# Choosing the first gather unit of a PEER layer in stages: best expert alone, then eight, then the rest

## The chip, the cores and the metric

The kernel runs on one core of one Trainium2 chip. The metric is the device time of one execution in microseconds (us); the median of three executions stands for the kernel. One execution was taken by the hardware profiler; its trace gives every number below. The engines are TensorE (PE in the profile), VectorE (DVE), ScalarE (ACT), GpSimd (POOL) and the queue engine SyncE (SP), and 16 DMA engines move data.

## The reference

The program computes two layers of a transformer trunk on 256 tokens of width 1024. Layer 0 mixes the tokens with a 2-D neighbourhood attention, layer 1 with a latent attention. After each mixer stand a layer norm and a product-key expert layer (PEER), then another layer norm. The expert layer is what matters here. For each token and each of 8 heads:

```
q = x @ w_q                       # two halves of 128
s = q . sub_keys                  # 2 x 128 scores
sv, si = top_k(s, 16)             # 16 best keys of each half
cand_s = sv[0][:, None] + sv[1][None, :]          # 16 x 16 sums
cand_i = si[0][:, None] * 128 + si[1][None, :]
best_s, pos = top_k(cand_s, 16)
e_idx = cand_i[pos]               # 16 experts of 16384
gate = softmax(best_s)
hid = gelu(x . u[e_idx])
y += sum(gate * hid * v[e_idx])
```

So each token of each layer reads 8 x 16 = 128 rows u and 128 rows v of a large table.

## The kernel before

The 256 tokens are two tiles of 128, one token to a partition. A group g is one head of one tile: 16 groups in a layer, 16 rows k in each, so 512 gathers in all (`row_no` numbers them). One gather (L1073, GpSimd, an indirect DMA) fetches for each of 128 tokens one expert's u and v, 8 KB a partition, 1.05 MB in all, into one of `RING` = 8 slots of the tile `uv`.

For every row VectorE computes the dot product with the token (`dot`, L1621, it reads `px` in PSUM), ScalarE applies Gelu to the results of two rows (`weigh`), VectorE multiplies by the gate (`weights`, L1627), ScalarE builds a diagonal matrix (L1228), and TensorE adds diagonal times v to the sums (`add`, L638). Three rows of group 0 (k = 5, 9, 13), and some of later groups, are added by VectorE instead (`add_on_vector`). A gather into a slot waits until the row eight before it has been added (`s_acc`, or `s_vrow`). In layer 0 the slots hold attention weights first, so the gathers n < 5 also wait for the projection "rest" n of TensorE (`rest_of_keys`, L362, and `rest_of_queries`, L370), and gather 7 waits for `rest_of_keys(6)` (`s_k6`).

There is no planner. Each engine has its own program, and within an engine the order is the order of the text. Pieces of side work (`side`) are tied to row numbers. VectorE chooses the experts of group g + 1 between the dots of group g: `key_top16` at one row, `pair_top16` two rows later, `expert_numbers` two after that, `gates` two after that. Group 0 of a layer has no rows to hide behind. `first_tile` does it in one piece: layer norm, `key_top16` (it waits for ScalarE's copy of the scores, `store_key_scores`, L1185), `pair_top16` (with the numbers of the first eight experts inside it), `expert_numbers` of the other eight, `gates`, and in layer 1 the rotation of the queries (`rope_q`, L1596).

The choice works so. MAX8 finds the eight largest of a row, FIND_INDEX8 their places, MATCH_REPLACE8 puts -1e30 over them, and a second MAX8 finds the next eight. The place `pos` of a pair in the 16 x 16 square is split into its two coordinates; each is compared with 0..15 (`hit`), the hits are multiplied by the key numbers and summed (`pick`), and first times 128 plus second plus the layer's offset is the expert's number.

GpSimd waits on `s_top8` before the gathers k = 0..7 of group 0 and on `s_top` before k = 8. In `first_tile(0)` TensorE's order is: rest 0, transposes of the norm, rest of keys 1, queries of group 0 (L536), half a seed (L348), key scores of group 0 into PSUM bank 7 (L548), rest of queries 1, rest 2 to 4, seed, `load_px` (L523), queries and key scores of group 1 (bank 7 again), rest of keys 6; then the rows. In layer 1 it is: queries 0, half a seed, key scores 0, two rotated-query products, seed, queries and scores of groups 1 and 2, `load_px`.

## Time and profile before

| | us |
|---|---|
| median of 3 executions | 1594.32 |
| lowest, highest | 1591.54, 1594.63 |
| profiled execution, its own time | 1593.75 |
| its span in the trace | 1591.9 |
| busy: PE, DVE, ACT, POOL | 1351.2, 1064.4, 488.0, 494.5 |
| first gather of layer 0, last of layer 0 | 125.63, 814.85 |
| first gather of layer 1, last of layer 1 | 904.56, 1568.51 |

The span counts from the first to the last instruction of the trace; the time of the execution is 1.85 us more. All times inside the program are from the span's start. "DMA share" is the mean busy share of the 16 DMA engines, "PEclk" the granted clock of TensorE as a part of 2.4 GHz.

### The profile page before, as it was taken

How to read it: one execution, taken by the hardware profiler on the slowest of the kernel's cores; microseconds unless marked ns; L12 is line 12 of the kernel's file. 1: busy time of each engine (PE TensorE's matmuls, PEld its weight loads, DVE VectorE, ACT ScalarE, POOL GpSimd, SP SyncE). 2: the span in 40 equal slices, each digit the busy share in tenths (PEclk: the TensorE clock that was granted, in tenths of full speed). 3: DMA queues.
4: the chain of work that ended last, by engine and by line, in shares of the span. 5: the costliest groups of instructions: out<-in, count | busy, mean ns of one | idle time of the engine just before them, and what ended most of it. 6: DMA issues, size and time to landing. Idle time of an engine off the chain costs nothing.

```text
span 1591.9 us, 16214 instructions
## 1 busy us (share of the span) xinstructions
PE 1351.2 (85%) x5046; PEld 733.5 (46%) x5046; DVE 1064.4 (67%) x2835; ACT 488.0 (31%) x1274; POOL 494.5 (31%) x524
## 2 busy tenths in 40 slices
PE   7999888888887888789889879988778988887877
PEld 7888534433354454444446634444334443333322
DVE  1127876778867877676653587777875876776765
ACT  1122342334323332223334233343332322222222
POOL 0003333334333333333320133343333333333331
PEclk9999998989998999999999989999999999999999
DMA  9528999999999999999993499999999999999996
GB/s 353 188 102 322 399 408 421 409 414 411 409 410 403 422 417 422 418 421 385 406 388 106 171 416 420 408 411 419 407 390 420 414 402 421 420 421 422 421 421 268
DMA packets 92821, 601.20 MB, mean 378 GB/s; under 512 B 10432, under 2 KB 12864, under 8 KB 26560
## 3 DMA queue, kind: packets, MB, share of 16 engines
q0 software_dynamic: 73728, 536.90, 82.2%
q1 hardware_dynamic: 19008, 63.28, 10.5%
q8 instruction: 40, 0.66, 0.2%
q14 instruction: 45, 0.37, 0.1%
HBM read 599.09 MB, written 1.05 MB: 377 GB/s over the span
## 4 chain that ended last, share of the span: by engine, by line
PE 37%; DMA 33%; DVE 22%; issue 3%; ACT 3%; DVEq 2%; POOL 0%; SPq 0%; POOLq 0%
DMA uv<-in_peer_uv_dram,expert 32%; PE y L638 19%; DVE uv L1621 11%; PE spare L536 3%; PE y L500 3%; PE px L353 2%; PE y L378 2%; ACT diag L1228 1%; DVE key_idx L1511 1%; DVE key_left L1503 1%; DVE key_idx L1505 1%; PE spare L395 1%; DVE wts L1627 1%; DVE key_top L1500 1%; DVE pos L1528 1%
## 5 line engine op out<-in xcount | busy, mean ns | idle before, releaser
L638 PE MATMUL y<-uv,diag 128*128 128x512 f32 x1888 | 912.9, 623 | 167.7 <-ACT diag L1228 166.9
L1621 DVE CUSTOM_DVE_ANT_0 uv<-px,uv 128x1024 f32<-128x1024 f32 x512 | 617.5, 1220 | 305.8 <-DMA uv<-in_peer_uv_dram,expert 299.6
L1073 POOL DMA_INDIRECT uv<-in_peer_uv_dram,expert x512 | 491.0, 959 | 1064.0 <-PE y L638 838.4
L638 PEld LDWEIGHTS y<-uv,diag 128*128 128x128 f32 x1888 | 349.5, 197 | 610.1 <-issue 341.6
L1228 ACT ACTIVATE diag<-ident,wts 128x128 f32<-128x128 f32 x472 | 166.3, 394 | 440.1 <-DVE wts L1627 430.9
L1220 ACT ACTIVATE act_hid<-hid 128x2 f32<-128x2 f32 x260 | 52.9, 203 | 482.4 <-DVE hid L1621 482.0
L1220 ACT ACT_TABLE_LOAD x54 | 69.3, 1283 | 1.0
L477 PE MATMUL spare<-ident,probs 128*128 128x128 f32 x96 | 16.9, 302 | 39.2 <-DVE probs L1448 35.8
L1640 DVE SCALAR_TENSOR_TENSOR vsum<-uv,wts,vsum 128x1024 f32<-128x1024 f32 x37 | 47.5, 1284 | 3.8 <-issue 0.5
L1627 DVE TENSOR_TENSOR wts<-act_hid,gate 128x2 f32<-128x2 f32 x260 | 40.6, 156 | 12.5 <-ACT act_hid L1220 12.4
L1621 DVE DVE_READ_ACCUMULATOR2_ANT hid<- 128x1 f32 x512 | 42.3, 83 | 0.0
L1190 ACT ACT_TABLE_LOAD x30 | 38.5, 1283 | 0.5
L1392 DVE TENSOR_TENSOR probs<-spare,bias 128x320 f32<-128x320 f32 x16 | 7.6, 473 | 45.4 <-PE spare L395 45.4
L477 PEld LDWEIGHTS spare<-ident,probs 128*128 128x128 f32 x96 | 11.4, 150 | 53.1 <-DVE probs L1448 52.5
L536 PEld LDWEIGHTS spare<-hT,wb_rows 128*128 128x128 f32 x256 | 30.6, 192 | 6.1 <-issue 6.1
L536 PE MATMUL spare<-hT,wb_rows 128*128 128x128 f32 x256 | 31.8, 277 | 0.0
L353 PE MATMUL px<-hT,uv 128*128 128x160 f32 (+1 forms) x176 | 24.6, 300 | 8.0 <-DMA uv<-in_na_w_dram 8.0
L500 PE MATMUL y<-wb_rows,oT 128*128 128x512 f32 x64 | 30.1, 592 | 0.0
L353 PEld LDWEIGHTS px<-hT,uv 128*128 128x128 f32 x176 | 24.1, 201 | 9.6 <-issue 9.6
L548 PEld LDWEIGHTS spare<-keysT,qT 128*128 128x128 f32 x128 | 18.7, 191 | 13.5 <-issue 11.5
L1540 DVE TENSOR_TENSOR hit<-pos_abf,iota 128x512 f32<-128x512 f32 (+1 forms) x34 | 22.5, 661 | 2.9 <-issue 0.4
L1543 DVE TENSOR_TENSOR hit<-hit,key_idxf 128x512 f32<-128x512 f32 (+1 forms) x34 | 22.5, 661 | 2.5
(268 smaller groups left out, 1272.6 us busy)
## 6 DMA issues: line engine op xcount, KB each, us to landing
uv<-in_peer_uv_dram,expert POOLq DMA_INDIRECT x512, 10.8
wb_rows<-in_peer_w_q_dram SPq DMA_DIRECT2D x16, 512.0 KB, 8.7
uv<-in_na_w_dram SPq DMA_DIRECT2D x11, 512.0 KB, 9.9
wb_rows<-in_na_w_out_dram SPq DMA_DIRECT2D x8, 512.0 KB, 9.0
uv<-in_mla_w_out_dram SPq DMA_DIRECT2D x8, 512.0 KB, 10.7
wb_rows<-in_mla_w_out_dram SPq DMA_DIRECT2D x8, 512.0 KB, 7.8
bias<-in_na_bias_dram SPq DMA_DIRECT2D x16, 160.0 KB, 7.5
w_vu<-in_na_w_dram SPq DMA_DIRECT2D x4, 512.0 KB, 8.6
```

Of the source, the lines that this page charges most:

```text
L353: last = T.matmul(B[b][:, 0:width], w[:, k, :], hT[:, k, 0:width], start=(k == 0), stop=(k == DK - 1))
L378: last = T.matmul(B[3][:, t * P:(t + 1) * P], hT[:, k, t * P:(t + 1) * P], w[:, k, :], start=(k == 0), stop=(k == DK - 1))
L500: last = T.matmul(Y[t][:, c, :], oT[n % 2][:, :], w[:, c * 512:(c + 1) * 512], start=False, stop=(j == PAIRS - 1))
L536: last = T.matmul(B[b][:, c * DKEY:(c + 1) * DKEY], w[:, k, :], hT[:, k, t * P:(t + 1) * P], start=(k == 0), stop=(k == DK - 1))
L638: last = T.matmul(Y[t][:, c, :], diag[:, n % RING, :], uv[:, n % RING, 1, c * 512:(c + 1) * 512], start=False, stop=(k == TOPK - 1 and g % ...
L1073: pool.indirect_dma_start(uv[:, n % RING, :, :].rearrange("p h d -> p (h d)"), None, uv_table, bass.IndirectOffsetOnAxis(ap=expert[:, g, k ...
L1190: A.activation(best_e[:, :], best_d[:, :], ACT.Exp).then_inc(s_be, 1)
L1220: A.activation(act_hid[:, first:end], hid[:, first:end], ACT.Gelu).then_inc(s_gelu, 1)
L1228: A.activation(diag[:, n % RING, :], ident[:, :], ACT.Copy, scale=wts[:, k:k + 1]).then_inc(s_diag, 1)
L1621: V_.tensor_tensor_reduce(out=rows, in0=px[:, :, :], in1=rows, scale=1.0, scalar=0.0, op0=ALU.mult, op1=ALU.add, accum_out=hid[:, k:k + 1] ...
L1627: V_.tensor_tensor(wts[:, first:end], act_hid[:, first:end], gate[:, g, first:end], ALU.mult).then_inc(s_wts, 1)
L1640: V_.scalar_tensor_tensor(out=vsum[:, :], in0=rows, scalar=wts[:, k:k + 1], in1=vsum[:, :], op0=ALU.mult, op1=ALU.add).then_inc(s_vrow, 1)
```

## The change

Group 0 of each layer is chosen by a new function, `first_choice`, that reads the key scores straight from PSUM bank 7. It is in stages. The eight best keys of each half are found, and with them the best pair, which is always the best key of one half with the best of the other: its number is stored and `s_best` raised, on which gather k = 0 now waits. Then the best eight pairs are sought in the 8 x 8 square of these keys, their numbers decoded with comparisons 8 wide, and `s_top8` raised for k = 1..7. After that bank 7 is given back, the second eight keys are found, the 16 x 16 square is made with the taken pairs covered, and the other eight pairs chosen. ScalarE's copy of group 0's scores is gone. For all groups the decoding is shorter: the multiplication by 128 and the offset are applied to the key numbers at once (`key_numbers`), the coordinates are compared as integers with no cast in between, and one sum over both halves gives the expert's number.

```diff
@@ -47,6 +47,7 @@
 START = 4
 QUADS = HEADS // 4
 FIRST = 204
+TOP = 8
 THROUGH = 6
 KEPT = 6
 SPAN = 160
@@ -158,9 +159,8 @@
         best = sb("best", [P, TOPK])
         pos = sb("pos", [P, TOPK], u32)
         pos_ab = sb("pos_ab", [P, 2, TOPK], u32)
-        pos_abf = sb("pos_abf", [P, 2, TOPK])
-        hit = sb("hit", [P, 2, TOPK, TOPK])
-        pick = sb("pick", [P, 2, TOPK])
+        hit = sb("hit", [P, TOPK * 2 * TOPK])
+        pick = sb("pick", [P, TOPK])
         best_d = sb("best_d", [P, TOPK])
         best_e = sb("best_e", [P, TOPK])
         ahead = sb("ahead", [P, 16])
@@ -203,7 +203,7 @@
         s_first_half = sem("first_half_of_sums_done"); s_var = sem("ln_var_ready"); s_std = sem("ln_std_ready"); s_xhat = sem("ln_xhat_ready")
         s_css = sem("latent_squares"); s_cstd = sem("latent_std"); s_cn = sem("latents_normed")
         s_q0 = sem("first_half_of_queries_done"); s_px = sem("px_ready")
-        s_bd = sem("best_minus_max"); s_be = sem("best_exp"); s_top = sem("experts_chosen"); s_top8 = sem("first_experts_chosen")
+        s_bd = sem("best_minus_max"); s_be = sem("best_exp"); s_top = sem("experts_chosen"); s_top8 = sem("first_experts_chosen"); s_best = sem("top_expert_chosen")
         s_uv = [sem(f"expert_rows_landed{i}") for i in range(RING)]
         s_dot = sem("dot_done"); s_gelu = sem("gelu_done"); s_wts = sem("weights_ready")
         s_vrow = sem("v_row_added_by_vector")
@@ -1057,10 +1057,12 @@
                     if g:
                         pool.wait_ge(s_top, layer * GROUPS + g + 1)
                     else:
-                        pool.wait_ge(s_top8, layer + 1)
+                        pool.wait_ge(s_best, layer + 1)
                     for k in range(TOPK):
                         n = row_no(layer, g, k)
-                        if g == 0 and k == 8:
+                        if g == 0 and k == 1:
+                            pool.wait_ge(s_top8, layer + 1)
+                        if g == 0 and k == TOP:
                             pool.wait_ge(s_top, layer * GROUPS + 1)
                         if n >= RING and row_on_vector(n - RING):
                             pool.wait_ge(s_vrow, vrow_no(n - RING + 1))
@@ -1313,7 +1315,6 @@
                     store_rest(0)
                 fetch_table(ACT.Exp)
                 store_queries(layer, 0, 6)
-                store_key_scores(layer, 0, 7)
                 if layer == 0:
                     store_rest(1)
                     store_rest(2)
@@ -1510,17 +1511,22 @@
                 for c in range(2):
                     V_.max_index(key_idx[:, c, 8:16], key_top[:, c, 8:16], key_left[:, c, :])
 
-            def pair_top16(layer=None):
-                V_.tensor_tensor(cand[:, :, :], key_top[:, 0, :].unsqueeze(2).broadcast_to([P, TOPK, TOPK]),
-                                 key_top[:, 1, :].unsqueeze(1).broadcast_to([P, TOPK, TOPK]), ALU.add)
-                V_.tensor_copy(key_idxf[:, :, :], key_idx[:, :, :])
+            def key_numbers(layer, some):
+                V_.tensor_scalar(key_idxf[:, 0, some], key_idx[:, 0, some], float(KEYS), float(layer * EXPERTS), ALU.mult, ALU.add)
+                V_.tensor_copy(key_idxf[:, 1, some], key_idx[:, 1, some])
+
+            def pair_sums(out, n):
+                V_.tensor_tensor(out, key_top[:, 0, 0:n].unsqueeze(2).broadcast_to([P, n, n]),
+                                 key_top[:, 1, 0:n].unsqueeze(1).broadcast_to([P, n, n]), ALU.add)
+
+            def pair_top16(layer):
+                pair_sums(cand[:, :, :], TOPK)
+                key_numbers(layer, slice(0, TOPK))
                 flat = cand[:, :, :].rearrange("p a b -> p (a b)")
                 dve.drain()
                 V_.max(best[:, 0:8], flat)
                 dve.drain()
                 V_.max_index(pos[:, 0:8], best[:, 0:8], flat)
-                if layer is not None:
-                    expert_numbers(layer, 0, slice(0, 8), s_top8)
                 V_.match_replace(cand_left[:, :], best[:, 0:8], flat, NEG)
                 dve.drain()
                 V_.max(best[:, 8:16], cand_left[:, :])
@@ -1529,25 +1535,62 @@
                 V_.tensor_tensor(best_d[:, :], best[:, :], best[:, 0:1].broadcast_to([P, TOPK]), ALU.subtract)\
                   .then_inc(s_bd, 1)
 
-            def expert_numbers(layer, g, some=slice(0, TOPK), done=s_top):
+            def expert_numbers(g, some, width, skip, done):
                 n = some.stop - some.start
-                dve.drain()
-                V_.tensor_scalar(pos_ab[:, 0, some], pos[:, some], 4, None, ALU.logical_shift_right)
-                V_.tensor_scalar(pos_ab[:, 1, some], pos[:, some], TOPK - 1, None, ALU.bitwise_and)
-                dve.drain()
-                V_.tensor_copy(pos_abf[:, :, some], pos_ab[:, :, some])
-                dve.drain()
-                V_.tensor_tensor(hit[:, :, some, :], pos_abf[:, :, some].unsqueeze(3).broadcast_to([P, 2, n, TOPK]),
-                                 iota16[:, :].unsqueeze(1).unsqueeze(1).broadcast_to([P, 2, n, TOPK]), ALU.is_equal)
-                dve.drain()
-                V_.tensor_tensor(hit[:, :, some, :], hit[:, :, some, :],
-                                 key_idxf[:, :, :].unsqueeze(2).broadcast_to([P, 2, n, TOPK]), ALU.mult)
-                dve.drain()
-                V_.tensor_reduce(pick[:, :, some], hit[:, :, some, :], X, ALU.add)
-                dve.drain()
-                V_.tensor_scalar(pick[:, 0, some], pick[:, 0, some], float(KEYS), float(layer * EXPERTS), ALU.mult, ALU.add)
-                dve.drain()
-                V_.tensor_tensor(expert[:, g, some], pick[:, 0, some], pick[:, 1, some], ALU.add).then_inc(done, 1)
+                hits = hit[:, 0:n * 2 * width].rearrange("p (n c a) -> p n c a", n=n, c=2)
+                dve.drain()
+                V_.tensor_scalar(pos_ab[:, 0, some], pos[:, some], 4 if width == TOPK else 3, None, ALU.logical_shift_right)
+                V_.tensor_scalar(pos_ab[:, 1, some], pos[:, some], width - 1, None, ALU.bitwise_and)
+                dve.drain()
+                V_.tensor_tensor(hits, pos_ab[:, :, some].rearrange("p c n -> p n c").unsqueeze(3).broadcast_to([P, n, 2, width]),
+                                 iota16[:, 0:width].unsqueeze(1).unsqueeze(1).broadcast_to([P, n, 2, width]), ALU.is_equal)
+                dve.drain()
+                V_.tensor_tensor(hits, hits, key_idxf[:, :, 0:width].unsqueeze(1).broadcast_to([P, n, 2, width]), ALU.mult)
+                dve.drain()
+                V_.tensor_reduce(pick[:, some], hits.rearrange("p n c a -> p n (c a)"), X, ALU.add)
+                dve.drain()
+                chosen = slice(some.start + skip, some.stop)
+                V_.tensor_copy(expert[:, g, chosen], pick[:, chosen]).then_inc(done, 1)
+
+            def first_choice(layer):
+                scores = [B[7][:, c * KEYS:(c + 1) * KEYS] for c in range(2)]
+                block, rest = vsum[:, 0:TOP * TOP], vsum[:, TOP * TOP:2 * TOP * TOP]
+                dve.wait_ge(s_full[7], job["ks", layer, 0])
+                for c in range(2):
+                    V_.max(key_top[:, c, 0:8], scores[c])
+                dve.drain()
+                for c in range(2):
+                    V_.max_index(key_idx[:, c, 0:8], key_top[:, c, 0:8], scores[c])
+                pair_sums(block.rearrange("p (a b) -> p a b", a=TOP), TOP)
+                dve.drain()
+                key_numbers(layer, slice(0, TOP))
+                V_.max(best[:, 0:8], block)
+                dve.drain()
+                V_.tensor_tensor(expert[:, 0, 0:1], key_idxf[:, 0, 0:1], key_idxf[:, 1, 0:1], ALU.add).then_inc(s_best, 1)
+                V_.max_index(pos[:, 0:8], best[:, 0:8], block)
+                expert_numbers(0, slice(0, TOP), TOP, 1, s_top8)
+                for c in range(2):
+                    last = V_.match_replace(key_left[:, c, :], key_top[:, c, 0:8], scores[c], NEG)
+                last.then_inc(s_free[7], 1)
+                V_.match_replace(rest, best[:, 0:8], block, NEG)
+                dve.drain()
+                for c in range(2):
+                    V_.max(key_top[:, c, 8:16], key_left[:, c, :])
+                dve.drain()
+                for c in range(2):
+                    V_.max_index(key_idx[:, c, 8:16], key_top[:, c, 8:16], key_left[:, c, :])
+                pair_sums(cand[:, :, :], TOPK)
+                dve.drain()
+                key_numbers(layer, slice(TOP, TOPK))
+                V_.tensor_copy(cand[:, 0:TOP, 0:TOP], rest.rearrange("p (a b) -> p a b", a=TOP))
+                dve.drain()
+                flat = cand[:, :, :].rearrange("p a b -> p (a b)")
+                V_.max(best[:, 8:16], flat)
+                dve.drain()
+                V_.tensor_tensor(best_d[:, :], best[:, :], best[:, 0:1].broadcast_to([P, TOPK]), ALU.subtract)\
+                  .then_inc(s_bd, 1)
+                V_.max_index(pos[:, 8:16], best[:, 8:16], flat)
+                expert_numbers(0, slice(TOP, TOPK), TOPK, 0, s_top)
 
             def gates(layer, g):
                 dve.wait_ge(s_be, layer * GROUPS + g + 1)
@@ -1664,9 +1707,9 @@
                         key_top16(layer, g + 1)
                     if k == first + 2:
                         dve.drain()
-                        pair_top16()
+                        pair_top16(layer)
                     if k == first + 4:
-                        expert_numbers(layer, g + 1)
+                        expert_numbers(g + 1, slice(0, TOPK), TOPK, 0, s_top)
                     if k == first + 6:
                         gates(layer, g + 1)
                 if at == 131:
@@ -1718,10 +1761,7 @@
                 norm_stats(mix0, 0, s_y, pair_no(layer, 0, PAIRS))
                 norm_scale(mix0, 0)
                 norm_store(mix0, 7)
-                key_top16(layer, 0)
-                dve.drain()
-                pair_top16(layer)
-                expert_numbers(layer, 0, slice(8, TOPK))
+                first_choice(layer)
                 gates(layer, 0)
                 if layer:
                     for half in range(2):
```

## Rows read from the trace of the kernel before

**Rows 1.** The page: busy time by engine, and DMA queue 0, the gathers.

```profile
PE 1351.2 (85%) x5046; PEld 733.5 (46%) x5046; DVE 1064.4 (67%) x2835; ACT 488.0 (31%) x1274; POOL 494.5 (31%) x524
...
q0 software_dynamic: 73728, 536.90, 82.2%
```

**Rows 2.** Windows: us, busy by engine, PEclk, DMA share, GB/s moved.

```profile
118.00:127.00 9.00, 9.00 (x83) 9.00 (x82) 7.62 (x36) 1.05 (x6) 1.09 (x1) 1.00 0.01 2
127.00:133.00 6.00, 6.00 (x56) 6.00 (x56) 3.52 (x12) 2.35 (x7) 4.75 (x5) 1.00 0.89 302
133.00:175.00 42.00, 36.38 (x198) 25.82 (x198) 31.00 (x84) 13.70 (x35) 11.29 (x13) 0.96 1.01 419
175.00:203.00 28.00, 26.31 (x110) 14.62 (x108) 23.78 (x69) 11.32 (x28) 10.49 (x12) 1.00 1.00 388
900.00:914.00 14.00, 9.58 (x74) 8.63 (x73) 10.23 (x38) 3.24 (x7) 7.30 (x8) 0.94 0.96 360
```

**Rows 3.** Line L1621, what the dots wait for in the whole trace.

```profile
  DMA uv<-in_peer_uv_dram,expert: 299.6, 237
```

**Rows 4.** Line L1073, the gathers.

```profile
DMA to landing us min/median/max: 5.5/10.8/17.0
```

**Rows 5.** Timeline of VectorE, layer 0, first choice.

```profile
118.17 0.49 DVE L1500 MAX8 key_top<-key_scores_sb 128x8 f32<-128x128 f32 x2 [5.75 <-ACT key_scores_sb L1185]
...
121.80 0.43 DVE L1519 MAX8 best<-cand 128x8 f32<-128x256 f32 x1
...
125.18 0.17 DVE L1550 TENSOR_TENSOR expert<-pick 128x8 int32<-128x8 f32 x1
...
126.73 0.15 DVE L1529 TENSOR_TENSOR best_d<-best 128x16 f32<-128x16 f32 x1
...
129.44 0.16 DVE L1554 TENSOR_REDUCE gate_s<-best_e 128x1 f32<-128x16 f32 x1
```

**Rows 6.** Groups of VectorE instructions by form: count, busy, mean ns.

```profile
L1540 DVE TENSOR_TENSOR hit<-pos_abf,iota 128x512 f32<-128x512 f32 x30 | 20.8, 693 | 2.6 <-issue 0.4
...
L1514 DVE TENSOR_TENSOR cand<-key_top 128x256 f32<-128x256 f32 x32 | 13.6, 425 | 2.9
...
L1596 DVE SCALAR_TENSOR_TENSOR rope_a<-px,cos_t 128x256 f32<-128x256 f32 x2 | 0.8, 424 | 0.2
...
L1538 DVE CAST pos_abf<-pos_ab 128x32 f32<-128x32 uint32 x30 | 5.5, 184 | 2.2
```

**Rows 7.** Timeline of TensorE, layer 0.

```profile
117.10 0.61 PE L548 MATMUL spare<-keysT,qT 128*128 128x128 f32 x4
...
124.67 1.98 PE L370 MATMUL y<-hT,uv 128*128 128x128 f32 x16
...
136.58 1.92 PE L362 MATMUL y<-hT,uv 128*128 128x96 f32 x16
...
169.97 0.63 PE L477 MATMUL spare<-ident,probs 128*128 128x128 f32 x4 [3.39 <-ACT qT L1178]
```

**Rows 8.** Timeline of GpSimd, layer 0, gathers 0 and 7.

```profile
125.63 1.09 POOL L1073 DMA_INDIRECT uv<-in_peer_uv_dram,expert  x1 [123.84 <-DVE expert L1550]
...
138.78 0.94 POOL L1073 DMA_INDIRECT uv<-in_peer_uv_dram,expert  x1 [4.51 <-PE y L362]
```

**Rows 9.** Timeline of VectorE, layer 0, the dots of rows 0, 4 and 12.

```profile
132.02 1.22 DVE L1621 CUSTOM_DVE_ANT_0 uv<-px,uv 128x1024 f32<-128x1024 f32 x1 [1.88 <-PE px L523]
...
143.15 1.23 DVE L1621 CUSTOM_DVE_ANT_0 uv<-px,uv 128x1024 f32<-128x1024 f32 x1 [2.02 <-DMA uv<-in_peer_uv_dram,expert]
...
167.52 1.23 DVE L1621 CUSTOM_DVE_ANT_0 uv<-px,uv 128x1024 f32<-128x1024 f32 x1 [1.16 <-DMA uv<-in_peer_uv_dram,expert]
```

**Rows 10.** Timeline, layer 1: VectorE, choice begins, rotation begins; GpSimd, gather 8.

```profile
897.10 0.49 DVE L1500 MAX8 key_top<-key_scores_sb 128x8 f32<-128x128 f32 x2 [5.75 <-ACT key_scores_sb L1185]
...
909.16 0.42 DVE L1596 SCALAR_TENSOR_TENSOR rope_a<-px,cos_t 128x256 f32<-128x256 f32 x1
...
925.13 0.94 POOL L1073 DMA_INDIRECT uv<-in_peer_uv_dram,expert  x1 [10.69 <-PE y L638]
```

## The prediction

> **What bounds the kernel now.** I read the page first. It shows TensorE busy for 85% of the span and VectorE for 67%, but the gathers alone take 82.2% of what 16 DMA engines have, for 536.9 MB in 512 gathers, 1.05 MB each [rows 1]. The windows by stage decide which is the limit: once gathers run, the DMA share is 1.00 or more and the engines move 388 to 419 GB/s, so a gather costs about 1.05/0.42 = 2.5 us [rows 2]. The dots, which come first in each row's chain, wait 237 times for a landing, 299.6 us in all [rows 3]. The chain of waits passes through landings, additions and dots by turns, since the ring has 8 slots: a gather lands 10.8 us after its issue in the middle, 5.5 us at best [rows 4], so most of that time is queue. The kernel is a stream of gathers, twice 256, with holes before the first of each layer. The hole is plain in layer 0: from 118 to 127 us the DMA share is 0.01 [rows 2], while VectorE makes the first choice. What starts the stream earlier shortens the kernel, as far as the stream does not run dry afterwards; so the reading is of the first choice, and then of what sets the issues behind it.
>
> **The first choice, step by step.** From the rows I take the time from one VectorE instruction to the next when a drain stands between them: 0.50 us for 256 elements, 0.36 for 128, 0.30 for 64, 0.25 for up to 32 (durations 0.693, 0.425, half of 0.49, 0.184 for 512, 256, 128 and 32 elements, plus about 0.07 to 0.08) [rows 5, 6]; the value for 64 is interpolated. Without a drain it is 0.08 to 0.15 less.
> Before, the scores are in PSUM at 117.71 [rows 7], ScalarE copies them, VectorE begins at 118.17, and the first eight experts are there at 125.18 + 0.17 = 125.35 [rows 5]; GpSimd issues gather 0 at 125.63 [rows 8], 0.28 later.
> After, VectorE begins at 117.75. To the best expert: two MAX8 0.55, two FIND_INDEX8 with their loads 0.54, the 8 x 8 sums 0.30, key numbers and MAX8 of 64 0.46, the sum 0.17, in all 2.02: 119.77, which is 5.6 us earlier. Gather 0 is issued at 120.05. To the eight: a search in 64 0.38, two coordinates 0.31, three passes of 128 1.08, a copy 0.17, in all 3.9 from the start: 121.65, which is 3.7 earlier. Then match and replace on 128, 128 and 64 0.9, MAX8 twice 0.55, indices 0.54, the square 0.50, numbers and the copy of 64 0.46, MAX8 of 256 0.50: the differences for the softmax are done after 7.4, at 125.15 against 126.88. Search 0.57 and decoding of eight 1.9 bring the gates to 9.8 after the start, 127.55 against 129.44 [rows 5]: VectorE is free 1.9 us earlier.
> At one place the Trainium skill speaks against the change. The rows show a pass over 256 elements out of PSUM at 424 ns and out of SBUF at 425 [rows 6], so reading in PSUM costs me nothing, and the copy saved is 0.42. The Trainium skill, VectorE: DVE Perf Modes, section Rules for kernel authors, advises to copy a matmul's output to SBUF first where many operations read it, and its table (section The TRN2 errata) gives PSUM sources 62 cycles more; as an estimate by that table six such passes would cost some 0.4 us and just cancel the saved copy. The row speaks against it.
>
> **What holds gathers 1 to 7 in layer 0.** GpSimd also waits for the projection "rest" n of TensorE. That chain is unchanged: one rest is some 1.8 us for keys and 1.8 for queries (the rows' 1.92 and 1.98 overlap their neighbours), so 3.57 from one to the next; the queries of rest 3 end at 124.67 + 1.98 = 126.65 [rows 7], those of rest 1, 2 and 4 at 119.5, 123.1 and 130.2. So the issues are 0 at 120.0, 1 at 121.9, 2 at 123.4, 3 at 126.9, 4 at 130.5, 5 at 131.8, 6 at 133.0. Gather 7 stays at 138.8: it waits for the rest of keys 6, which ends at 136.58 + 1.92 [rows 7, 8]. The head start of 5.6 us is thus one of gather 0, and shrinks to 0.3 by gather 4.
> It isn't lost for that, for the queue at the time was long: the dot of row 4 still waited for DMA at 143.15 [rows 9], 12 us after its issue. I look at what releases the dot of row 12 at 167.52, with 1.16 us of idleness before it, and TensorE's transposes behind it at 169.97 (the label names ScalarE; it is the normalising behind that dot), with 3.39 idle [rows 7, 9]. Three chains lead there.
> DMA: between 127 and 167.5 it moved 6 x 302 + 34.5 x 419 = 16.3 MB [rows 2]. After, gathers 0 to 7, 8.4 MB, trickle from about 121.5 with few in flight and are in by 144.5 (gather 7's issue and 5.5 to 6). The other 7.9 MB take 18.9 us at 419 or 20.3 at 388: row 12 at 163.4 to 164.8, a gain of 2.7 to 4.1.
> VectorE: its waits for DMA before rows 1 to 4 (6.1 us in four, the longest 2.02) and 12 (1.16), 7.3 us, may go, less 1.6 for the first Gelu, which stands on ScalarE behind the copies of group 1: up to 6.1 with the shorter decoding. The first dot stays at 132.02, for it waits for `px` [rows 9].
> TensorE: 0.71 and 1.05 of waits for diagonals and the 3.39: at most 5.2.
> So the DMA decides; I take 4.0. With the wait of 3.39 shrunk to about 1, TensorE should not fall to 1.2 GHz there. The granted clock of 0.96 over 42 us is 1.7 us lost at this one place [rows 2], on the engine that then binds up to 203 (26.3 of 28 busy, DMA at 388). I take 1.0 of it: **layer 0 gains 5.0**, bounds 2.5 and 7.
> The nearest row on a thin queue is the ramp, 302 GB/s against 419 [rows 2]. The Trainium skill, DMA: Bandwidth & Descriptors, section Bandwidth, gives 341 GB/s to a single 1 MB transfer and 425 to 16 MB; the trace agrees in direction, and by its rate, as an estimate, the seven gathers 0 to 6 would take 21.5 us and still be in before gather 7.
>
> **Layer 1.** The gathers' stream starts at 904.56, but weight loads already fill the DMA from 900: 360 GB/s up to 914, 2.0 us lost against 419 [rows 2]. Gather 8 at 925.13 waits 10.69 us for the addition of row 0 [rows 10], and that hangs on VectorE: choice, gates, rotation at 909.16, `px`, dot 0, the keys of group 1, dots 1 and 2. At 925 less than three gathers' worth is queued, so gather 8 must be earlier too. The choice begins 0.41 earlier and is shorter by 1.5: 1.9 for all of this. The DMA can give back at most the 2.0. **Layer 1 gains 1.9**, bounds 0.9 and 2.9. Bank 7 is given back 4.4 us after the start, about 901.1; TensorE wants it for group 1 at 903.4 (in layer 0 at 136, with 14 us to spare).
>
> **The other 30 groups.** A cast and a multiplication with their drains go, 0.25 each, and a small instruction comes, 0.08: 0.42 us of VectorE less per group, 12.6 in all [rows 6]. Mostly it lies beside the DMA stream and is worth nothing; it counts where VectorE's bursts (choice between dots) run the ring low. In such a stretch the DMA fell to 388 [rows 2]. I take a twelfth, **1.0**; bounds 0 and 4. Comparing integers with floats at other than one element a cycle is unseen; the nearest row is 693 ns for 512 floats.
>
> **Sum.** 5.0 + 1.9 + 1.0 = 7.9 us. The profiled execution's 1593.75 becomes 1585.9; the median is 0.6 above it, so 1586.5.
>
> **Rivals.**
> A: only VectorE's end counts. If the ring's refill at gather 8 follows VectorE in both layers, the early gathers merely wait in their slots: 1.9 twice, 1590.5. For it: gathers 7 to 11 in layer 0 are paced by TensorE. Against it: the dot of row 12 waited for DMA. 0.16.
> B: the decoding counts. If every burst binds, half of the 12.6 us comes out on top: 1580. For it: dips in each stage; against it: shares at 1.00. 0.08.
> C: no gain. The DMA runs dry between 133 and 165 so far that layer 0 gives nothing, and layer 1 gives 1.9 less a thin queue: 1593. 0.07.
> D: slower. The comparison of integers with floats runs at half rate: 0.69 more per group against 0.42 saved, 0.27 x 30 = 8 us of VectorE. Against the 6.9 us of the two layers it ends above the old time only if more than six sevenths of that lies bare: all of it, with some 0.5 more in each first choice, gives 1594.3 - 6.9 + 8.1 + 1 = 1596.5. For it: nothing in the rows; against it: VectorE's share of 67%. 0.03.
> My forecast and its neighbours between 1583 and 1589: 0.66.
>
> **Range and chances.** Below lies B, above C and part of A. 1582 to 1591.5 leaves out about 2 in 10. A measurement tells 0.2%, 3.2 us, from no change: faster means under 1591.1. Forecast, B and most of A lie there, 0.85; C, the rest of A and half of D 0.12; slower 0.03.
>
> **What would show it.** Gather 0 at about 120.0 and 899.0; gather 3 held to 126.9 by L370, gather 7 still at 138.8. Gates at 127.5 and 906.5. The dot of row 12 near 163.5, the clock not falling at 170. Gather 8 of layer 1 near 923.2. Line L1540's successor at 693 ns. I'd be wrong if the DMA share between 130 and 160 fell well under 1, if row 12's dot stayed near 166, or if the last gather of layer 0 moved by less than 2.5.

## The result, and the profile after

The changed kernel takes 1583.21 us (median of 4 executions; 1581.96 to 1584.26), the kernel before 1592.93 beside it: ratio 0.993, with a 95% interval of [0.9911, 0.9949]. The same kernel, measured a second time, gave 1582.73 against 1593.22, 0.9945 [0.993, 0.996]. The times of the runs below are medians, with the ratio to the kernel before on the same chip and its interval. The forecast was 1586.5: the direction holds, and the gain is about 10 us where 7.9 were summed.

The profiled execution took 1584.26 us, its span 1582.2, against 1591.9. First the page of the kernel after, beside [rows 1]:

```profile
PE 1346.5 (85%) x5046; PEld 733.6 (46%) x5046; DVE 1055.6 (67%) x2809; ACT 487.1 (31%) x1272; POOL 497.9 (31%) x524
...
q0 software_dynamic: 73728, 536.90, 82.4%
```

The limits are the same and the gathers move the same bytes; VectorE is busy 8.8 us less. Windows of the kernel after (columns as in [rows 2]; the attention stage ran 1.07 us longer this time, so each window of layer 0 begins a microsecond later than its twin):

```profile
119.00:128.00 9.00, 9.00 (x84) 9.00 (x83) 7.73 (x43) 2.57 (x8) 2.99 (x4) 1.00 0.57 204
128.00:134.00 6.00, 6.00 (x56) 6.00 (x55) 2.15 (x6) 0.69 (x4) 2.80 (x3) 1.00 0.98 375
134.00:168.60 34.60, 30.93 (x177) 22.02 (x175) 27.32 (x77) 12.61 (x32) 12.64 (x12) 1.00 1.00 397
168.60:200.00 31.40, 29.92 (x132) 17.34 (x132) 26.20 (x70) 11.87 (x29) 11.49 (x11) 1.00 0.99 395
900.00:914.00 14.00, 3.62 (x19) 3.03 (x17) 8.84 (x31) 2.46 (x5) 2.09 (x2) 0.78 1.02 424
914.00:926.00 12.00, 11.24 (x29) 5.06 (x29) 11.05 (x32) 4.98 (x10) 4.18 (x4) 0.83 0.91 350
```

The hole of 9 us at a share of 0.01 now carries 204 GB/s. But the 35 us behind the ramp move 397 GB/s where they moved 419, at a share of 1.00: part of the head start goes back there. A run below, `one_wait`, says more about it. VectorE's first choice in layer 0, beside [rows 5]:

```profile
118.81 0.50 DVE L1560 MAX8 key_top<-spare 128x8 f32<-128x128 f32 x2 [5.33 <-PE spare L548]
...
120.67 0.16 DVE L1569 TENSOR_TENSOR expert<-key_idxf 128x1 int32<-128x1 f32 x1
...
122.56 0.17 DVE L1553 CAST expert<-pick 128x7 int32<-128x7 f32 x1
...
126.03 0.17 DVE L1590 TENSOR_TENSOR best_d<-best 128x16 f32<-128x16 f32 x1
...
128.59 0.33 DVE L1597 TENSOR_REDUCE gate_s<-best_e 128x1 f32<-128x16 f32 x1
```

From the start that is 1.86, 3.75, 7.22 and 9.78 us to the first expert, the eight, the differences and the gates; it was 8.56 and 11.27 to the last two. GpSimd's gathers 0, 1, 2, 3, 7 and 18, beside [rows 8]:

```profile
121.11 1.09 POOL L1075 DMA_INDIRECT uv<-in_peer_uv_dram,expert  x1 [119.31 <-DVE expert L1569]
123.01 0.94 POOL L1075 DMA_INDIRECT uv<-in_peer_uv_dram,expert  x1 [0.80 <-DVE expert L1553]
124.41 0.94 POOL L1075 DMA_INDIRECT uv<-in_peer_uv_dram,expert  x1 [0.46 <-PE y L370]
127.98 0.94 POOL L1075 DMA_INDIRECT uv<-in_peer_uv_dram,expert  x1 [2.63 <-PE y L370]
...
139.84 0.94 POOL L1075 DMA_INDIRECT uv<-in_peer_uv_dram,expert  x1 [4.86 <-PE y L362]
...
172.98 1.61 POOL L1075 DMA_INDIRECT uv<-in_peer_uv_dram,expert  x1 [5.54 <-PE y L638]
```

The dots of rows 0 and 12, beside [rows 9]: the first still waits for `px`, the other for a landing.

```profile
133.09 1.23 DVE L1664 CUSTOM_DVE_ANT_0 uv<-px,uv 128x1024 f32<-128x1024 f32 x1 [3.60 <-PE px L523]
...
166.13 1.23 DVE L1664 CUSTOM_DVE_ANT_0 uv<-px,uv 128x1024 f32<-128x1024 f32 x1 [1.71 <-DMA uv<-in_peer_uv_dram,expert]
```

Layer 1, beside [rows 10]: the choice and the rotation begin, ScalarE copies the queries of group 2, TensorE builds `px`, the first dot, and gather 8.

```profile
889.71 0.50 DVE L1560 MAX8 key_top<-spare 128x8 f32<-128x128 f32 x2 [5.33 <-PE spare L548]
900.43 0.42 DVE L1639 SCALAR_TENSOR_TENSOR rope_a<-px,cos_t 128x256 f32<-128x256 f32 x1
904.18 0.38 ACT L1180 ACTIVATE qT<-spare 128x256 f32<-128x256 f32 x1 [6.54 <-remote]
905.63 1.92 PE L523 MATMUL px<-ident,hT 128*128 128x128 f32 x8
907.58 1.22 DVE L1664 CUSTOM_DVE_ANT_0 uv<-px,uv 128x1024 f32<-128x1024 f32 x1 [4.55 <-PE px L523]
919.00 0.94 POOL L1075 DMA_INDIRECT uv<-in_peer_uv_dram,expert  x1 [16.50 <-PE y L638]
```

**Where the 9.7 us of span went.** I count from the end of each layer's key scores on TensorE (117.71 and 896.65 before, 118.78 and 889.68 after) to the last dot of each layer (827.12 and 1580.08 before, 821.84 and 1570.30 after). The attention stage lost 1.07; from the scores to the last dot of layer 0 the gain is 6.35 (709.41 less 703.06); layer 1, counted in the same way, took 683.4 before and 680.6 after, 2.8; the stage between the layers was 1.7 shorter. The change does not touch this last stage. There TensorE ran most of one product at 1.2 GHz in the profiled execution before (granted clock 0.57 in 837 to 841 us) and at 2.4 after:

```profile
836.62 6.24 PE L558 MATMUL y<-w_latkv,hT 128*128 128x320 f32 x16 [1.50 <-ACT hT L1095]
```
```profile
831.34 4.54 PE L558 MATMUL y<-w_latkv,hT 128*128 128x320 f32 x16 [1.50 <-ACT hT L1097]
```

So single traces carry 1 to 2 us there that aren't the change's. Layer 0 varies more: from the scores to its last dot it took 703.1 us in this trace, 705.7 in the changed kernel's second one, and 704.7 and 706.9 in two traces of it with idle ScalarE instructions added (`act_pad`, `pad_later`). Layer 1 varies less, 679.0 to 681.1 in the same four. The verdicts below therefore go by the medians.

### The profile page after: what moved, and what is told of

Same layout as the page of the kernel before. It is cut to its first block, busy times and chain, and to the rows that moved or that the text cites. A ratio compares the mean times of both kernels' runs of the same rounds, so it can differ in the third digit from the quotient of the medians.

```text
span 1582.2 us, 16120 instructions
## 1 busy us (share of the span) xinstructions
PE 1346.5 (85%) x5046; PEld 733.6 (46%) x5046; DVE 1055.6 (67%) x2809; ACT 487.1 (31%) x1272; POOL 497.9 (31%) x524
## 4 chain that ended last, share of the span: by engine, by line
PE 39%; DMA 31%; DVE 20%; ACT 4%; issue 4%; DVEq 1%; another core or an unknown queue 0%; POOL 0%; SPq 0%; POOLq 0%; ACTq 0%
DMA uv<-in_peer_uv_dram,expert 31%; PE y L638 19%; DVE uv L1664 10%; PE spare L536 4%; PE y L500 3%; PE px L353 2%; PE y L378 2%; ACT diag L1230 1%; DVE key_idx L1512 1%; DVE key_left L1504 1%; PE y L370 1%; PE y L362 1%; DVE key_idx L1506 1%; PE spare L395 1%; DVE wts L1670 1%
## 5 line engine op out<-in xcount | busy, mean ns | idle before, releaser
L548 PE MATMUL spare<-keysT,qT 128*128 128x128 f32 x128 | 20.3, 282 | 4.9 <-ACT qT L1180 4.4
L1548 DVE TENSOR_TENSOR hit<-hit,key_idxf 128x512 f32<-128x512 f32 (+2 forms) x34 | 22.2, 653 | 2.9 <-issue 0.4
## 6 DMA issues: line engine op xcount, KB each, us to landing
uv<-in_mla_w_out_dram SPq DMA_DIRECT2D x8, 512.0 KB, 10.5
```

Source lines behind the costliest of these rows:

```text
L548: last = T.matmul(B[b][:, c * KEYS:(c + 1) * KEYS], qT[:, c, :], keysT[:, 2 * layer + c, :], start=True, stop=True)
```

## The experiments

**The two halves apart.** `decode_only` is the kernel before with only the shorter decoding for groups 1 to 15; `choice_only` is the changed kernel with the long decoding in those groups.

```diff
-                        pair_top16()
+                        pair_top16_short(layer)     # decode_only; choice_only does the reverse
...
-                        expert_numbers(layer, g + 1)
+                        expert_numbers_short(g + 1)
```

> The kernel before with the shorter decoding in the 30 groups that lie between dots; the first choice of each layer stays as before. If these groups are hidden behind the stream of gathers, as the prediction had it, the time falls by about 1 us. If they account for what the prediction fell short by, it falls by 3 to 4 us, most of it in layer 1 and in steps, where the ring had run low.

> The changed kernel with the long decoding put back in the 30 other groups. Theory hidden decoding: some 9 us faster than before (the whole change less 1). Theory exposed decoding: 6 us faster. Gather 0 stays at about 2.3 us after the key scores. A third: if the 3.5 us in which ScalarE stood still in layer 1 belongs to the early gathers, it is seen here too.

Measured: 1588.77 against 1592.93, 0.9976 [0.9962, 0.9989]; and 1585.71, 0.9966 [0.9952, 0.998]. By the medians the halves are worth 4.2 and 7.2, 11.4 together, near the 9.7 to 10.5 of the whole. The decoding alone is worth 1.8 to 6.1 us by its interval; counted the other way, choice alone against the whole (1583.21 and 1582.73, and 1583.1 for `act_pad` on the same chip), 2.5 to 3. The choice alone is worth 3.2 to 7.6 by its interval. The comparison of integers took as long as that of floats:

```profile
L1545 DVE TENSOR_TENSOR hit<-pos_ab,iota 128x512 f32<-128x512 uint32 x30 | 20.8, 693 | 2.2
```

How much shorter VectorE's work became can be read from the traces: from the dot of row 0 of a group to that of row 7, waits taken off, the kernel before takes 0.38 us longer than the changed one (median of 26 groups; the groups at the ends and the middle of a layer are left out). Over 30 groups that is 11.5 us, an estimate, near the 12.6 of the prediction, and the gain is a quarter to a third of it.

**The head start taken away.** Gathers 0 to 7 wait for all sixteen experts; VectorE's program stays the changed one.

```diff
-                        pool.wait_ge(s_best, layer + 1)
+                        pool.wait_ge(s_top, layer * GROUPS + 1)
...
-                        if g == 0 and k == 1:
-                            pool.wait_ge(s_top8, layer + 1)
-                        if g == 0 and k == TOP:
-                            pool.wait_ge(s_top, layer * GROUPS + 1)
```

> The changed kernel, only that gathers 0 to 7 wait for the end of the whole first choice. VectorE's work is the same. If the head start of the gathers counts, they start 7.9 us later and the kernel loses 4 to 6 us in layer 0 and about 2 in layer 1 against the changed one: about 1590. If only VectorE's end counts (rival A), it stays at 1583.

Measured: 1592.53, 0.9999 [0.9986, 1.0012]: the whole gain is gone. Gather 0 is at 128.49, and the dot of row 0 waits for its landing, no longer for `px`:

```profile
134.28 1.23 DVE L1660 CUSTOM_DVE_ANT_0 uv<-px,uv 128x1024 f32<-128x1024 f32 x1 [5.46 <-DMA uv<-in_peer_uv_dram,expert]
```

The kernel before issued gather 0 at 125.63. So the run says that a late start of the stream costs; it does not say that the change's gain is its head start. No run issues the gathers when the kernel before did, with VectorE's new program. The choice also frees VectorE earlier, and how the 5.5 to 7.2 us of the first choice divide between the two is not shown.

**The stage for the best pair taken away.** Gather 0 waits for the first eight like gathers 1 to 7.

```diff
-                        pool.wait_ge(s_best, layer + 1)
+                        pool.wait_ge(s_top8, layer + 1)
...
-                        if g == 0 and k == 1:
-                            pool.wait_ge(s_top8, layer + 1)
```

> The changed kernel, but gather 0 waits for the first eight experts, like gathers 1 to 7; the best pair's expert has no stage of its own any more. In the profile of the changed kernel gather 0 is issued at 121.11 and gather 1 at 123.01, while the first dot waits for the token's projection in PSUM until 133.1, 12 us after the issue. Theory (the queue is shallow before 128 and refills under TensorE's gates): gather 0 at about 122.9, 1 at 124.0, 2 at 125.1, then as before; at most 0.4 us of DMA work is moved per layer, no more than +1 us in all, 1583 to 1584.5 beside 1583 for the changed kernel. Rival (each us of head start counts once per layer): two layers by 1.9 us, +3.8, about 1587.

Measured: 1582.15, 0.9932 [0.9909, 0.9955]. Gather 0 left at 123.07, 2.0 us later, gather 3 at 128.07 and gather 7 at 139.93 as ever. The first stage is worth nothing that can be measured. The windows at the same distance from the scores show what became of its head start:

```profile
119.06:128.06 9.00, 9.00 (x84) 9.00 (x82) 7.72 (x43) 2.58 (x9) 2.97 (x3) 1.00 0.33 118
134.06:168.66 34.60, 32.66 (x192) 23.76 (x191) 28.33 (x79) 12.82 (x33) 11.93 (x12) 1.00 1.01 420
```

Up to 128 us this kernel moves 0.8 MB less than the changed one (118 against 204 GB/s over 9 us), and from 134 on 0.8 MB more (420 against 397 over 34.6 us). The traces divide in the same way, 15.2 to 49.8 us behind the scores: in the twelve in which gather 0 goes out ahead of the others the stretch shows 391 to 399 GB/s, and in the four in which it doesn't 417 to 420. Why the rate differs at a share of 1.00 stays open.

**Other slots first.** In layer 0 the rows are gathered in the order 0, 5, 6, 1, 2, 3, 4, 7, since slots 5 and 6 wait for no projection.

```diff
-                    for k in range(TOPK):
+                    order = [0, 5, 6, 1, 2, 3, 4] + list(range(7, TOPK)) if (layer, g) == (0, 0) else list(range(TOPK))
+                    for i, k in enumerate(order):
...
-                        if g == 0 and k == 1:
+                        if g == 0 and i == 1:
```

> The changed kernel with the first gathers of layer 0 in the order 0, 5, 6, 1, 2, 3, 4, 7: slots 5 and 6 hold no attention weights, so these two need not stand behind the projections that hold gathers 3 and 4. If the thin queue between 122 and 137 us costs stream time, this gives 1 to 2.5 us: 1581.5. If the issues from gather 7 on, which TensorE paces, decide alone, nothing: 1583.

Measured: 1585.38, 0.9965 [0.9949, 0.9981], no better than the changed kernel. Seven issues were out by 131.72, but the issue of row 7 stayed at 140.01, and the dot of row 12 came at 165.61, 46.7 us after the scores, within the 45.6 to 47.4 of the traces with the staged choice and the order unchanged. What left earlier were rows that VectorE needs late; row 1 left at 125.66 where it left at 123.01, row 3 at 129.18 and row 4 at 131.72. This order gains nothing.

**The scores copied to SBUF again.**

```diff
+                store_key_scores(layer, 0, 7)
...
-                scores = [B[7][:, c * KEYS:(c + 1) * KEYS] for c in range(2)]
+                scores = [key_scores_sb[:, 0, c, :] for c in range(2)]
...
-                dve.wait_ge(s_full[7], job["ks", layer, 0])
+                dve.wait_ge(s_free[7], job["ks", layer, 0])
...
-                last.then_inc(s_free[7], 1)
```

> The changed kernel, but ScalarE copies the scores of group 0 to SBUF again and the staged choice reads them there; bank 7 is given back by the copy. Theory from the rows (a pass out of PSUM is as fast as one out of SBUF): the choice starts 0.42 us later in each layer and its steps last the same, MAX8 pair 0.49 to 0.50; +0.8 us at most, 1583 to 1584.5. Rival (the rule of the Trainium skill, VectorE: DVE Perf Modes, that many readings of PSUM are dearer than one copy): the six passes are shorter by 0.06 us each, so the experts are there at the same time as in the changed kernel and the time is the same or lower; it would show as MAX8 pairs under 0.45 us.

```profile
119.33 0.49 DVE L1561 MAX8 key_top<-key_scores_sb 128x8 f32<-128x128 f32 x2 [5.75 <-ACT key_scores_sb L1187]
```

Measured: 1583.51, 0.9939 [0.9916, 0.9962], the same as with PSUM read. The pair of MAX8 takes 0.49 from SBUF and 0.50 from PSUM, and the wait is 0.42 longer. Reading in place costs nothing that shows, and the 0.42 us saved is too little to show in the medians.

**Does VectorE's work count by its place?** Four small copies with a drain each, about 1.0 us, are added in every group but the last of a layer, which makes 30: right behind the decoding (`dose_burst`), or six rows later (`dose_idle`). A burst here is a stretch of VectorE's choosing between two dots.

```diff
+                    if k == first + 4:              # dose_idle: min(first + 10, TOPK - 1)
+                        for i in range(4):
+                            dve.drain()
+                            V_.tensor_copy(ballast[:, i, :], iota16[:, :])
```

> The changed kernel with four copies of 16 numbers more on VectorE (1.0 us with their drains) in each of the 30 other groups, right behind the decoding, 30 us in all. If such work in the bursts is exposed by a third, as decode_only says (4 of 12.6 us), it costs 9 to 12 us: 1593. If it is hidden as predicted (a twelfth), 2.5 us: 1586.

> The same four copies, but six rows later, where no choice is made and VectorE waits for landings. Theory burst: the place decides, and here they cost under 3 us: 1583 to 1586. Rival: VectorE's total work decides, wherever it stands: as dose_burst.

Measured beside a changed kernel of 1582.73: 1597.04, 1.0027 [1.0013, 1.0042], and 1587.64, 0.997 [0.9955, 0.9986]. In the traces the copies add 1.16 us to a group's rows 0 to 7 in the first kernel and 1.03 to its rows 8 to 14 in the second (medians of 26 groups, waits taken off), some 35 and 31 us in all. So they cost 14.3 in one place and 4.9 in the other, in the first more than either expectation had. From that I took the theory that VectorE's uninterrupted stretches between dots empty the ring, and two ways to make them less harmful.

**Shorter stretches.** The same choice in six pieces behind six dots, not three behind every second (`piece`, whose body is left out here, holds the instructions).

```diff
-                    if k == first:
-                        key_top16(layer, g + 1)
-                    if k == first + 2:
-                        dve.drain()
-                        pair_top16(layer)
-                    if k == first + 4:
-                        expert_numbers(g + 1, slice(0, TOPK), TOPK, 0, s_top)
+                    if first <= k < first + 6:
+                        piece(k - first, layer, g + 1)
```

> The changed kernel with the same instructions of the choice for groups 1 to 15 (some drains more), in six pieces behind six dots in place of three behind every second dot, so that no stretch of VectorE between two dots is longer than about 1.9 us where it was 3. Theory (VectorE's bursts empty the chain from addition to issue, so their length decides: 4 copies right behind a burst cost 14.3 us, six rows later 4.9): the time falls by 3 to 8 us, 1575 to 1580. Rival 1 (what counts is VectorE's work between a gather's landing and the last moment for its addition, in sum, not in bursts): no change, 1582 to 1585. Rival 2 (weights of two rows are late more often, as they now stand behind a piece at every row): slower, 1586.

Measured: 1593.84, 1.001 [0.9992, 1.0027], 11 us slower than the changed kernel, where 3 to 8 faster was expected. Dots of rows 48 and 55 (rows 0 and 7 of group 3), of the kernel after and of this one:

```profile
264.56 1.22 DVE L1664 CUSTOM_DVE_ANT_0 uv<-px,uv 128x1024 f32<-128x1024 f32 x1 [1.48 <-DMA uv<-in_peer_uv_dram,expert]
...
284.76 1.22 DVE L1664 CUSTOM_DVE_ANT_0 uv<-px,uv 128x1024 f32<-128x1024 f32 x1
```
```profile
264.71 1.23 DVE L1708 CUSTOM_DVE_ANT_0 uv<-px,uv 128x1024 f32<-128x1024 f32 x1 [1.48 <-DMA uv<-in_peer_uv_dram,expert]
...
286.28 1.22 DVE L1708 CUSTOM_DVE_ANT_0 uv<-px,uv 128x1024 f32<-128x1024 f32 x1
```

20.20 against 21.57: the pieces have drains of their own, and the passes over the two halves no longer stand side by side. 1.37 us is more than most groups show: with waits taken off the median of 26 groups is 1.03, some 31 us in all. 11 of the 31 reach the end, a third, though no stretch is long any more. As the edit added so much work, it doesn't test the length of the stretches by itself; short stretches did not save what they cost.

**The same work, later.** The decoding moves from row 4 to row 8 of a group; in `apart` also the square from row 2 to 4 and the gates from 6 to 10.

```diff
-                    if k == first + 4:
+                    if k == max(first + 4, 8):
                         expert_numbers(g + 1, slice(0, TOPK), TOPK, 0, s_top)
```

> The changed kernel, but the decoding of the next group's experts stands behind the dot of row 8 in place of row 4 (row 10 in the group before the second tile, as before); nothing else is moved, and VectorE has the same work. In the trace of the changed kernel VectorE runs through rows 0 to 6 of a group with no wait for DMA and waits before nearly each of the rows 7 to 15. Theory (the place counts: work in rows 0 to 7 delays additions and thus issues, work in rows 8 to 15 fills waits; four copies cost 14.3 us in the one place and 4.9 in the other): the decoding's 3.0 us per group become mostly covered, 3 to 12 us faster than the changed kernel, 1571 to 1580. Rival (the sum counts wherever it stands, and the dose's two places differed because one of them made the next gathers' list of experts late): 1581 to 1585. It is slower than that if the list of experts, now ready some 8 us later, holds the gather of the next group's row 0.

> The kernel with the late decoding, and also the square's choice moved from row 2 to row 4, the gates from 6 to 10, and ScalarE's exponential for the gates from the second to the fourth pair of rows, so that the pieces stand at rows 0, 4, 8 and 10 of a group instead of 0, 2, 4 and 6. Theory (place counts): another 0 to 4 us faster than the late decoding alone. Rival (sum counts): 1581 to 1585 like the changed kernel.

Measured: 1583.19, 0.9945 [0.9927, 0.9962], and 1583.52, 0.9944 [0.9925, 0.9964]: no difference from the changed kernel that would stand out of intervals of some 3 us to each side. No gather waited for the list of experts in either, bar the first two of each layer. Moving whole pieces between rows 2 and 10 is neutral; the amount of work isn't. The theory of the place falls for this work.

**ScalarE's pause in layer 1.** In the kernel after, ScalarE copies the queries of group 2 at 904.18, though TensorE had ended them at 900.69 (3.74 from 896.95), and `px` and the first dot stand behind that. The trace names no releaser in the program ("remote"), and one packet of the instruction queue moved in 898 to 908 us (packets, MB, share):

```profile
q8 instruction: 1, 0.02, 0.6%
```

`act_pad` adds 32 tiny copies on ScalarE before the attention, `pad_later` scatters them over groups 8 to 11 of layer 1.

```diff
+            for i in range(32):
+                A.activation(pad[:, i:i + 1], eps_col[:, :], ACT.Copy)
             store_k(0)
```

> The changed kernel with 32 small ScalarE instructions more at its very start, where ScalarE waits for the first weights (they write a tile that nothing reads). If ScalarE's 3.5 us of standing still in layer 1 come from the place in its instruction stream, they move or vanish, and dot 256 comes 2 to 2.5 us earlier against the key scores: time 1 to 2 us less. If they come from the data or a semaphore, they stay at the same copy of queries.

> The changed kernel with 32 tiny copies on ScalarE (0.2 us each) scattered over groups 8 to 11 of layer 1, so that ScalarE's program is the same up to there. The kernel with the same 32 copies near the start lost the pause of 6.5 us before ScalarE's copy of the queries of group 2 in layer 1 (it shows 904.18, 6.54 idle in the changed kernel, and TensorE's projection and the first dot come 3 us later by it). Theory (the pause hangs on where in ScalarE's program that copy lies, as with instructions loaded in pieces): the pause is there as in the changed kernel, first dot of layer 1 near 907.6. Rival (it hangs on the size of the program as a whole, or falls at random): no pause, first dot near 904.6. Time in all 1582 to 1585 either way.

Measured: 1583.1, 0.9947 [0.993, 0.9963], and 1583.47, 0.994 [0.9917, 0.9962]. Both lack the pause, and the second one has the same ScalarE program up to there. The pause is in the traces of the changed kernel (twice), of both doses and of the other slots, and in none of the other ten. `one_wait`, `decode_late` and `choice_only` have ScalarE's program of the changed kernel up to there and lack it. So the place in that program does not decide, and that explanation falls; nor does the early issue of the gathers, which `choice_only` has too. The padding is not shown to have removed the pause, for the traces go by the occasion: the four measured together (the changed kernel's second run, the doses, the other slots) all have it, and the ten measured on three other occasions all lack it. What makes the pause stays open. It costs the first dot of layer 1 3.3 us (15.6 after gather 0's issue in the kernel after, 12.3 in `act_pad`). Without it that dot and gather 8 are earlier:

```profile
904.64 1.23 DVE L1667 CUSTOM_DVE_ANT_0 uv<-px,uv 128x1024 f32<-128x1024 f32 x1 [1.25 <-PE px L524]
916.13 0.94 POOL L1076 DMA_INDIRECT uv<-in_peer_uv_dram,expert  x1 [13.28 <-PE y L639]
```

From the scores (890.03 in `act_pad`) layer 1 takes 679.0 us to its last dot here, 679.4 in `one_wait` and 679.5 in `pad_later`, against 680.6 and 681.1 in the two traces of the changed kernel, which have the pause. So it seems to cost the end 1 to 2 us.

**The changed kernel again**, beside the doses and the other slots:

> The changed kernel unchanged, beside the others on the same chip. Both theories: about 1583. It says whether ScalarE's standing still for 3.5 us in layer 1 comes back: if it belongs to the place in the instruction stream it is seen again, if it was an accident of one execution it isn't.

Measured 1582.73, as told above, and its trace has the pause again. No version here beats it by more than the intervals.

## Why the prediction was right or wrong

**The failed step is the last term of the sum, "the other 30 groups".** It priced 12.6 us less of VectorE's work at "a twelfth, 1.0", and it is 3 to 4: 4.2 for the decoding alone (1.8 to 6.1 by the interval, which leaves out 1.0), 2.5 to 3 for its absence. This is also what the whole sum lacks, 7.9 against 9.7 to 10.5. The work itself was sized well, 11.5 us for 12.6. The bounds of 0 and 4 about hold (one of the measurements is 4.2); the choice inside them was wrong. The reason given, that the work lies "beside the DMA stream and is worth nothing", rests on a share of 1.00. The rows were there to doubt it: 299.6 us of waits for landings in 237 dots [rows 3] are 1.3 a dot, and the other 275 dots waited for no landing. In group 3 of the kernel after, rows 1 to 7 run through 20 us with no wait, then nearly every row waits. It would fit that in such a half VectorE sets when rows are added and slots freed, and that the wait behind it gives back only part. But this is argued, not shown, and `decode_late` speaks against it, since moving the decoding into the half with waits gained nothing. The size is shown; why it is a quarter to a third stays open. Rival B had this mechanism and too large a share, half. Measured shares are 0.22 to 0.37 for the decoding, 0.36 for the pieces, 0.41 and 0.16 for the added copies.

**The first choice on VectorE: right.** To the steps 2.02, 3.9, 7.4 and 9.8 answer 1.86, 3.75, 7.22 and 9.78 (the first three are starts, their instruction of 0.17 to add). Hit comparison 693 ns, as before. Taking the 1.07 of the attention stage off, gather 0 was due at 121.1 and came at 121.11, gather 3 at 127.97 and came at 127.98, gather 7 at 139.85 and came at 139.84. That the first stage's head start shrinks to 0.3 us by gather 4 was said; `one_wait` shows that nothing of it is left in the time.

**Layer 0: the 5.0 is not settled.** The trace of the kernel after gains 6.35 from the scores to the last dot, with the decoding's part in it, some 2 us if it falls on both layers alike. But the four traces named above run from 703.1 to 706.9, against one trace of the kernel before with 709.4, so the gain is 2.5 to 6.4 by the choice of trace. "The dot of row 12 near 163.5" is 45.8 us after the scores. It came 47.4 after them in this trace and 46.3, 45.6, 45.6 and 46.8 in those of `choice_only`, `act_pad`, `one_wait` and `pad_later`; before it was 49.8. That is a gain of 2.5 to 4.2, where the working had 2.7 to 4.1 and took the upper end. The rate of 397 GB/s lies inside the 388 to 419 of the working and isn't the reason for the late dot here: `act_pad` has 397 too. The gain grows behind that dot: in the trace of the kernel after gather 18 came 4.1 earlier and row 40's dot 5.7, counted from the scores.

The clock did not fall at 170 in this trace, but it did, to 1.2 GHz, in the changed kernel's second one and in `pad_later`:

```profile
169.00:171.50 2.50, 2.50 (x11) 1.98 (x11) 1.31 (x3) 0.14 (x2) 0.00 (x0) 0.50 1.02 423
```

These are the two traces with 705.7 and 706.9 us for layer 0; the kernel after and `act_pad`, at full clock there, have 703.1 and 704.7. So a term of the size of the 1.0 is likely, but the fall isn't reliably avoided as the prediction had it. No run shows the term by itself.

**Layer 1: the term of 1.9 was too small where the pause is absent.** In the trace of the kernel after the gain is only 2.8 with the decoding's part in it, since `px` waited behind ScalarE's pause: the dot of row 0 came 17.90 after the scores, 0.9 later than before (16.98), and gather 8 waited 16.50 for the addition of row 0, where it waited 10.69. Nothing in the rows of before announced the pause. Without it, in `act_pad`, that dot comes 14.61 after the scores, 2.4 earlier than before, and gather 8 26.1, also 2.4 earlier, where 1.9 was said for both. To the last dot `choice_only` takes 679.6, 3.8 less than the kernel before, and `act_pad`, `one_wait` and `pad_later` take 2.8 to 3.2 less than `decode_only` (682.3). So the first choice gave some 2.8 to 3.8 in this layer, against a term of 1.9 with an upper bound of 2.9. "Gather 8 of layer 1 near 923.2" can't be held against the 919.00 as it stands: less the 6.97 that the scores came earlier, 919.00 is 0.8 later than before's 925.13, not 1.9 earlier.

For both layers' first choices together the medians give 5.5 to 7.2 where the terms made 6.9. If layer 1 gave 2.8 to 3.8 of it, layer 0 gave 1.7 to 4.4 and not 5.0, and the two errors cancel: the sum is then right by luck. With one trace of the kernel before, this is likely and not shown.

**Rivals.** A: that only VectorE's end counts falls in its strong form, by `late_issue`: 1592.53, where A would have had 1583. Of gather 0 it is true that the head start gives nothing. Whether the other gathers' earlier issue, against that of the kernel before, gives anything beyond VectorE's earlier end was not tested; A's 3.8 for the first choice lies inside the interval of `choice_only`. C is excluded by the interval. D: the comparison ran at full rate. The rule of the Trainium skill (VectorE: DVE Perf Modes, Rules for kernel authors) on copying PSUM first did not show its price: 0.50 against 0.49 us for the MAX8 pair, and medians that agree.

## What to carry to other kernels

A DMA share of 1.00 over 40 us does not make another engine's work free: count how many of its steps wait for nothing. In this kernel a saving of VectorE's work was worth a quarter to a third of it, 3 to 4 us of 11.5. Find out which gate in front of the stream really decides: the stage for a single expert gave nothing, as the seven other slots were gated elsewhere. A small added load in each place tells what work costs there, but it is no law of place: two such runs differed by a factor of three, and moving the real work the same way did nothing. And take several traces before a term is judged by one: layer 0 varied by 4 us among four traces of nearly the same program.

## What the runs showed that I had not expected

- Four copies per group cost 14.3 us behind row 4 and 4.9 behind row 10, yet the decoding of 3.0 us, moved from row 4 to row 8, neither cost nor gave anything. The two don't fit one simple rule, and no run here settles it.
- With gather 0 issued alone ahead, the stream later moves 397 GB/s at a full share, and 420 at the same place when the first gathers leave one behind another. It isn't the thin queue as such, for `one_wait` has it too (118 GB/s up to 128 us). The cause is open.
- ScalarE stood still 3.5 us longer than its operand needed, in 5 of the 15 traces other than before's, beside a full DMA (share 1.02). Neither its program ahead of that place nor a wait that the trace names explains it; four of the five were measured together.
